# Hybrid encoder step: input columns in a new order, the convolution norm moved to its projection, a first norm that starts from tokens

## The reference

```
mod = silu(c) @ w_ada + b_ada                 # 6 x 1024, for each of two groups
h = rms_norm(x, g_norm1) * (1 + sc1) + sh1
a_in, b_in, q, k, v, qi, ki, wi, gl = split_cols(h @ w_in)
a = a_in[:, :1024] * sigmoid(a_in[:, 1024:])  # GLU
a = causal_dwconv(concat(hist, a), w_dw, b_dw)          # 31 taps
y_a = silu(layer_norm(a, ln_c_g, ln_c_b)) @ w_pa
z = gelu(b_in);  u = z[:, :1024]
vg = layer_norm(z[:, 1024:], ln_v_g, ln_v_b)
y_b = (u * spatial_gate(vg, w_s, b_s)) @ w_pb           # 128 x 128 masked mixing in 8 groups
q, k = rms_norm(q, g_q), rms_norm(k, g_k)
score = sum_h wi * relu(qi @ ki^T)                      # indexer: picks up to 256 keys a query
o = softmax(q @ k^T - slope * dist, on the picked keys) @ v;  y_c = o @ w_pc
m = sigmoid(gl)[0] * y_a + sigmoid(gl)[1] * y_b + sigmoid(gl)[2] * y_c
x = x + g1 * (m @ w_o)
x = x + g2 * (squared_relu(modulated rms_norm(x) @ w_1 + b_1) @ w_2 + b_2)
```

## Time and profile before

| | us |
|---|---|
| median of 3 runs (2717.16 to 2717.63) | 2717.55 |
| the profiled execution | 2716.72 |
| its span | 2714.9 |
| PE busy | 2508.3 (92%) |
| DVE busy | 1237.8 (46%) |
| POOL busy | 1223.2 (45%) |
| ACT busy | 676.9 (25%) |

### The profile page before, as it was taken

The page is one execution under the profiler, slowest core; times in us unless marked ns, Lnnn a source line. Parts: engine busy times, 40 slices in busy tenths (PEclk is TensorE's granted clock), DMA queues, the critical chain, the costliest instruction groups (busy, mean ns, idle before and its releaser), DMA issues.

```text
span 2714.9 us, 37116 instructions
## 1 busy us (share of the span) xinstructions
PE 2508.3 (92%) x14178; PEld 2345.9 (86%) x14178; DVE 1237.8 (46%) x2190; ACT 676.9 (25%) x824; POOL 1223.2 (45%) x611
## 2 busy tenths in 40 slices
PE   7798979999999997968789999999799999999998
PEld 7698858999999996946344999998699999999998
DVE  1421259999999995154667112211521222222212
ACT  2222463222444234212545100001401100100110
POOL 2532201222988564810222455555644544554552
PEclk7799989999999999965899999999899999999999
DMA  7112202332232232123100457441011111111112
GB/s 273 34 51 61 92 27 70 116 116 86 96 96 85 91 96 93 55 67 100 32 16 5 146 179 244 142 150 39 24 48 36 47 50 38 39 50 43 38 43 86
DMA packets 241682, 217.22 MB, mean 80 GB/s; under 512 B 10529, under 2 KB 220547, under 8 KB 241341
## 3 DMA queue, kind: packets, MB, share of 16 engines
q1 hardware_dynamic: 205780, 127.29, 15.8%
q10 hardware_dynamic: 35817, 88.84, 9.5%
HBM read 163.90 MB, written 52.20 MB: 80 GB/s over the span
## 4 chain that ended last, share of the span: by engine, by line
PE 62%; issue 20%; DVE 7%; POOL 7%; ACT 2%; DMA 1%; SPq 0%; POOLq 0%; DVEq 0%; ACTq 0%
PE acc L1683 52%; PE acc L1977 2%; POOL st L625 1%; POOL wlo L580 1%; PE acc L1651 1%; DVE mx L1535 1%; POOL whi L535 1%; PE acc L1928 1%; PE acc L1695 1%; PE acc L1952 1%; POOL wlo L590 1%; PE acc L1923 1%; DVE st L1531 1%; DVE probs L1531 1%; DMA x1T<-xT_d 0%
## 5 line engine op out<-in xcount | busy, mean ns | idle before, releaser
L1683 PE MATMUL acc<-xa,whi 128*128 128x364 f32 x4176 | 1045.4, 332 | 11.6 <-ACT zT L915 5.4
L1683 PEld LDWEIGHTS acc<-xa,whi 128*128 128x128 f32 x4176 | 747.4, 190 | 20.1 <-issue 17.7
L1683 PE MATMUL acc<-xa,wlo 128*128 128x364 f32 x2088 | 690.4, 331 | 0.0
L1683 PE MATMUL acc<-xb,whi 128*128 128x364 f32 x2160 | 534.9, 329 | 2.7 <-POOL wlo L538 2.7
L535 POOL TENSOR_TENSOR whi<-raw,one 128x1024 fp32r<-128x1024 f32 (+2 forms) x153 | 241.4, 1577 | 514.2 <-PE acc L1683 510.2
L1683 PEld LDWEIGHTS acc<-xa,wlo 128*128 128x128 f32 x2088 | 396.8, 190 | 0.0
L1683 PE MATMUL acc<-xf,whi 128*128 128x364 f32 x1536 | 382.1, 330 | 6.3 <-issue 6.3
L1683 PEld LDWEIGHTS acc<-xb,whi 128*128 128x128 f32 x2160 | 383.1, 188 | 3.0 <-POOL wlo L538 3.0
L1683 PE MATMUL acc<-xb,wlo 128*128 128x364 f32 x1080 | 354.8, 328 | 0.0
L538 POOL TENSOR_TENSOR wlo<-raw,whi 128x1024 fp32r<-128x1024 f32 (+2 forms) x153 | 313.6, 2050 | 12.0
L1683 PEld LDWEIGHTS acc<-xf,whi 128*128 128x128 f32 x1536 | 273.0, 189 | 6.6 <-issue 6.6
(11 more groups left out here) (273 smaller groups left out, 2809.7 us busy)
## 6 DMA issues: line engine op xcount, KB each, us to landing
raw<-in_w_in_dram SPq DMA_DIRECT2D x72, 512.0 KB, 4.1
wmod<-in_w_ada_dram SPq DMA_DIRECT2D x32, 512.0 KB, 4.4
...
gate_d<-st ACTq DMA_DIRECT2D x24, 546.0 KB, 2.8
st<-gate_d ACTq DMA_DIRECT2D x24, 546.0 KB, 4.9
m_d<-st ACTq DMA_DIRECT2D x16, 546.0 KB, 3.6
st<-m_d ACTq DMA_DIRECT2D x16, 546.0 KB, 5.9
```

What stands on the lines that cost most here:

```text
L1683: last = nc.tensor.matmul(acc[0:m, s, c, 0:CW], w[:, s, k, 0:m], x[:, half, k, CW * c:CW * (c + 1)], start=(k == 0 and p == 0), stop=(k == ...
```

## The change

- The columns of the input projection are taken in another order: indexer, scores, GLU, gates, the first four u tiles (`UA`), then k, v, q, then VG, then the other four u tiles (`UB`). The convolution's sums are made beside the first u tiles; the means of the convolution stand ahead of VG, those of v between the second and the third tile of UB.
- The convolution's rows go to `ya_d` raw. Mean and root go to `ml_d` and are loaded again before PC; in PB, DVE subtracts and multiplies each row, and ACT does Swish and the rounding.
- The weight tiles of u, k, v, q and VG are rounded by ACT (`round_next`); POOL makes the remainder.
- The first head means of k wait for the convolution (`conv_ok`), because the buffers are shared.
- In the mix DVE multiplies from PSUM, and the copy on ACT is gone. The bias comes by a matmul over eight partitions. The six additions of the distance to the masks (L1444) go into the mask's last step.
- At the start SP loads x first, then the first weights and `w_ada`; the 15 parameter loads are ACT's. ACT squares x by tokens with a sum in the same instruction, DVE evicts all transposes. Conditioning is made in four groups of 16 matmuls of 256 columns, two groups ahead of the first projection and one each behind its rows 1 and 3; ACT scales and shifts the rows.

```diff
-N_GLU = N_Q + H
-N_GATE = N_GLU + 2 * KT
-N_U = N_GATE + 3 * KT
-N_VG = N_U + KT
-N_PC = N_VG + KT
+N_VG = N_Q + H
+N_UB = N_VG + KT
...
+            sp.dma_start(x_tile(0), x_rows[0]).then_inc(x_ld[0], 16)
+            for i, to in enumerate((st[:, 1:3, 0:D], x_mid[:, 0:2, :], x_mid[:, 2:4, :])):
+                rows_of = x_prompt[0, P * (2 * i + 1):P * (2 * i + 3), :]
+                sp.dma_start(to, rows_of.rearrange("(t p) d -> p t d", p=P)).then_inc(x_ld[i + 1], 16)
+            for t in (7, 8):
+                sp.dma_start(x_tile(t), x_rows[t]).then_inc(x_ld[4], 16)
...
+            for q in range(ADA1 // 2):
+                for s in (q, ADA1 // 2 + q):
+                    sp.dma_start(wada[:, s], v_ada[:, :, 2 * P * s:2 * P * (s + 1)]).then_inc(ada_ld[s], 16)
...
-            load_run(N_KV, win, 2 * NKV, C_K)
-            load_run(N_Q, win, H, C_Q)
...
-            load_run(N_U, win, KT, C_U)
+            load_run(N_U, win, UA, C_U)
+            load_run(N_KV, win, 2 * NKV, C_K)
+            load_run(N_Q, win, H, C_Q)
             load_run(N_VG, win, KT, C_V)
+            load_run(N_UB, win, KT - UA, C_U + UA * P)
...
+            def c_sums(n):
+                for m, part in enumerate((apad[:, SUM_ROWS[n], 0:NT], stage(3 + n % 2))):
+                    pool.wait_ge(ln_sq, n + 1)
+                    pool.wait_ge(c_add, 2 * n + m + 1)
+                    total = (sum_a, sum_b)[m][:, :]
+                    nc.gpsimd.tensor_tensor(total, total, part, ALU.add).then_inc(c_add, 1)
...
+            act.dma_start(st[0:CONV_W, 3, 0:D], w_dw[0]).then_inc(par_ld, 16)
...
+                ins = nc.scalar.activation(acc[0:rows(t), 1, 0:2, :].rearrange("p c n -> p (c n)"), x_tile(t), ACT.Square,
+                                           accum_out=ssq[0:rows(t), t:t + 1])
...
+            def partial_sums(q):
+                for s in range(2):
+                    act.wait_ge(ada_mm, 4 * q + s + 1)
+                    nc.scalar.activation(msb1[:, s, :], aux[:, s, 0:2 * P], ACT.Copy).then_inc(mod_cp, 1)
+            def shifted(k):
+                h = 1 + 3 * (k % 2)
+                act.wait_ge(xn_ok, k + 1)
+                act.wait_ge(mod_ok, 2 * (k // 2) + 2)
+                if k > 1:
+                    act.wait_ge(h_lo, k - 1)
+                for g, (a, b) in enumerate(((0, SEQ), (SEQ, NT))):
+                    ins = nc.scalar.activation(st[:, h, a:b], st[:, 2 * (k % 2), a:b], ACT.Identity,
+                                               bias=mod[:, g, M_SH1 + k:M_SH1 + k + 1], scale=gain1[:, g, k:k + 1])
+                ins.then_inc(h_ok, 1)
+                act.wait_ge(h_ok, k + 1)
+                nc.scalar.activation(xa[:, 0, k, :], stage(h), ACT.Copy).then_inc(h_hi, 1)
+            partial_sums(0)
+            partial_sums(1)
+            for q in range(ADA1 // 2):
+                for k in (2 * q, 2 * q + 1):
+                    shifted(k)
+                if q + 2 < ADA1 // 2:
+                    partial_sums(q + 2)
...
+            def round_next(n, s):
+                act.wait_ge(w_load[s], 8 * (n - s) + 32)
+                nc.scalar.activation(whi[:, s], raw[:, s], ACT.Copy).then_inc(w_hi, 1)
...
+                    row = apad[:, SUM_ROWS[n], 0:NT]
+                    wait(act, c_add, 2 * n if n > 1 else 0)
+                    nc.scalar.activation(stage(3 + n % 2), row, ACT.Square).then_inc(ln_sq, 1)
+                    act.dma_start(ya_d[SUM_ROWS[n]], row).then_inc(ya_st, 16)
...
+            def qk_tile(n, s, idx):
+                act.wait_ge(prod, n + 1)
+                round_next(n, s)
...
+                if k == 1:
+                    act.wait_ge(ln_ok, 1)
+                    for m in range(2):
+                        act.dma_start(ml_d[m], stage(2 + m)).then_inc(ml_st, 16)
...
-                        nc.scalar.activation(mixed[:, j, a:b], acc[:, j, m, 0:b - a], ACT.Copy).then_inc(mix_ev, 1)
...
-                        act.wait_ge(br_ld[j], 16 * (i + (KT // 2 * b + 1)))
+                        if b == 0:
+                            act.wait_ge(br_ld[j], 16 * (i + 1))
+                        else:
+                            act.wait_ge(lnc_n, 2 * i + (j + 1))
+                            row = st[:, 2 + j:3 + j, 0:NT]
+                            nc.scalar.activation(row, row, ACT.Silu, bias=par[:, bass.ds(2 * i + (R_LCB + j), 1)],
+                                                 scale=par[:, bass.ds(2 * i + (R_LCG + j), 1)]).then_inc(lnc_s, 1)
+                            act.wait_ge(lnc_s, 2 * i + (j + 1))
...
+            for m, to in enumerate((mean_c, rstd_c)):
+                act.dma_start(to[:, :], ml_d[m]).then_inc(ml_ld, 16)
...
+            def scaled(k):
+                if k > 1:
+                    dve.wait_ge(h_ok, k - 1)
+                nc.vector.tensor_tensor(stage(2 * (k % 2)), xT[:, k, :], acc[:, 1, :, :].rearrange("p c n -> p (c n)")[:, 0:NT],
+                                        ALU.mult).then_inc(xn_ok, 1)
+            dve.wait_ge(x_evd, TT + 1)
+            dve.wait_ge(sq_mm, 1)
+            scaled(0)
+            scaled(1)
+            for q in range(ADA1 // 2):
+                conditioning(q)
+                if q:
+                    scaled(2 * q)
+                    scaled(2 * q + 1)
...
-            with dve.Fori(0, KT // 2) as i:
-                for j in range(2):
-                    row = apad[:, bass.ds(2 * i + j, 1), 0:NT]
-                    nc.vector.tensor_tensor(row, row, st[:, 2:3, 0:NT], ALU.subtract).then_inc(lnc_c, 1)
-                    dve.wait_ge(lnc_c, 2 * i + (j + 1))
-                    nc.vector.tensor_tensor(row, row, st[:, 3:4, 0:NT], ALU.mult).then_inc(lnc_n, 1)
...
-                    nc.vector.tensor_tensor(row, row, mixed[:, j, 0:NT], ALU.mult).then_inc(yb_ok, 1)
+                    nc.vector.tensor_tensor(row[:, 0:TOK], row[:, 0:TOK], acc[:, j, :, :].rearrange("p c n -> p (c n)")[:, 0:TOK],
+                                            ALU.mult).then_inc(yb_ok, 1)
...
+                        if b == 1:
+                            row = st[:, 2 + j:3 + j, 0:NT]
+                            dve.wait_ge(br_ld[j], 16 * (i + (KT // 2 + 1)))
+                            nc.vector.tensor_tensor(row, row, mean_c[:, :].unsqueeze(1), ALU.subtract).then_inc(lnc_c, 1)
+                            dve.wait_ge(lnc_c, 2 * i + (j + 1))
+                            nc.vector.tensor_tensor(row, row, rstd_c[:, :].unsqueeze(1), ALU.mult).then_inc(lnc_n, 1)
...
-            def first_modulation(m):
-                pe.wait_ge(ada_ld[m // 2], 16)
-                for k in range(KT):
-                    last = nc.tensor.matmul(acc[:, 0, 0, 2 * m:2 * m + 2], wada[:, m // 2, k, P * (m % 2):P * (m % 2 + 1)],
-                                            cT[:, :, k], start=(k == 0), stop=(k == KT - 1))
-                if m % 2:
-                    last.then_inc(ada_mm, 1)
...
+            def conditioning(q):
...
+                for s, chunk in ((0, q), (1, ADA1 // 2 + q)):
+                    pe.wait_ge(ada_ld[chunk], 16)
+                    for k in range(KT):
+                        c = k % 4
+                        last = nc.tensor.matmul(aux[32 * c:32 * (c + 1), s, 0:2 * P], cpad[:, k, :], wada[:, chunk, k, :],
+                                                start=(k < 4), stop=(k >= 4))
+                    last.then_inc(ada_mm, 1)
+                for s in range(2):
+                    pe.wait_ge(mod_cp, 2 * q + s + 1)
+                    for h in range(2):
+                        last = nc.tensor.matmul(aux[:, s, 2 * P + 2 * h:2 * P + 2 * h + 2], msb1[:, s, P * h:P * (h + 1)],
+                                                sel[:, :], start=True, stop=True)
...
-            gemm_as_ready(N_KI, 0, xa, h_lo, 0, KIW)
+            conditioning(0)
+            conditioning(1)
+            for k in range(KT):
+                if k == 0:
+                    pe.wait_ge(w_split, N_KI + 1)
+                pe.wait_ge(h_lo, k + 1)
+                for c in range(CH):
+                    for p, (w, half) in enumerate(((whi, 0), (whi, 1), (wlo, 0))):
+                        last = nc.tensor.matmul(acc[0:KIW, 0, c, 0:CW], w[:, 0, k, 0:KIW], xa[:, half, k, CW * c:CW * (c + 1)],
+                                                start=(k == 0 and p == 0), stop=(k == KT - 1 and p == 2))
+                if k in (1, 3):
+                    conditioning(k // 2 + 2)
...
             plain(N_KV + 1)
+            pe.wait_ge(conv_ok, POOL_ROWS[0])
             key_means(0)
...
+            for k in range(KT - UA):
+                if k < 2:
+                    pe.wait_ge(ev_act, N_UB + k - 1)
+                elif k == 2:
+                    pe.wait_ge(ev_act, N_UB + 2)
+                    pe.wait_ge(v_add, 2 * KT + 2)
+                    layer_norm_means()
+                    pe.wait_ge(ln_mean, 2)
+                else:
+                    pe.wait_ge(ln_var, 2)
...
```

(47 more changed lines are left out.)

647 lines of the change are left out of this document (294 added, 353 removed).

## The result

The changed kernel takes 2683.64 us (median of four runs, 2681.62 to 2690.5) against 2717.59 of the kernel before beside it: a ratio of 0.9871, with 0.9859 to 0.9883 as its 95% interval, or 34 us less. The forecast was 2698, 20 less. The profiled execution took 2681.62, its span 2679.7; PE's last matmul ends at 2676.24, and at 2711.41 before: 35.2 to account for.

The account below looks back on a forecast made before the run. PE was taken to set the end, by its matmuls where full and its waits elsewhere. From 2716.72, -26 (start) -7 (order) -2 (mix) +15 (PB) = -20 gave 2696.7, with 0.83 to the median 2697.5, forecast 2698; own range 2682 to 2713.

Parts of the forecast that it names:

- PB: Second branch projection: convolution-norm subtract and multiply on DVE close a loop, turn 14.4 over PE's 12.0; +15 us.
- Start: Before the first index-query tile: x loaded first, squares on ACT, conditioning in groups; 94 us against 119.7, -26.
- the break: In the start, ACT's row loop waits for partial sums of conditioning groups 2 and 3; 8.5 us each, 17 together.
- The rival of a start that gives little: Start: parameters late beside x, breaks of 15; first index-query tile at 112 in place of 94, total 2716; chance 0.12.
- Order: New column order, from the end of the index-query tiles to the mix: 1007.8 us against 1015.3, -7.
- The 8 added for twelve more tiles to round: First head means to last q tile: 8 us added for ACT rounding twelve more weight tiles and a 0.94 clock.
- the stall: After the two k tiles, PE waits 17.5 us for the convolution and the sums whose buffers the k norm uses.
- nothing makes the convolution end sooner against the scores: New order: DVE's convolution keeps its distance from the scores while PE arrives earlier, eating most of the norms' gain; total -7.
- Mix: Spatial mix: PSUM copy goes, DVE multiplies from PSUM, evictions stay; half clock, gain between 0 and 7.7, -2 us.
- the rival of a full clock: Spatial mix holds full clock behind twelve full gemms: about 60 us for 84.9, total 2675; chance 0.17.
- The rival of 19: Second branch projection: DVE's new instructions meet POOL every turn, turn 19, cost +45 to +49, total 2729; chance 0.15.
- Taken at nothing: Attention, output projection and MLP keep their instructions, and the reload of the two statistics lies beside other work: 0 us.

## Why the prediction was right

The sign, the mechanisms of the start, the mix and PB, and the order of the terms held; the sum was 15 short, from terms that were sized too dear and from a search that ran shorter by chance.

- **Start**, -26 forecast, -29.0. The parameters came at 21.37 for 18, the first row at ACT at 50.48 for 50, so what lies between took 29.1 for 32. From there to the first index-query tile it took 40.2 for 43.4: the mis-sized term is the break, about 7.2 where 8.5 was taken, twice. The rival of a start that gives little (112) is out.
- **Order**, -7 forecast, -14.6. The scores took 63.6 for 55.9, since POOL's work on the GLU weights now comes in among them, behind SP's wait for the outputs; the forecast named no such move. The 8 added for twelve more tiles to round was not needed: v to the last q tile took 179.3 for 186.7. That these two cancel is luck. Most of what is left lies between GLU's start and the head means, 595.1 for 601.4: GLU (220.2 for 221.8), the gate, u and k tiles (360.8 for 362.1) and the stall (14.1 for 17.5). VG with its rest took 157.1 for 158. Here "nothing makes the convolution end sooner against the scores" did not hold in the profiled execution: the convolution ends 583.3 after GLU's start, and ended 589.6 after it before. The search's tiny instructions took 31.7 for 39.1, and the forecast had no term for that. Where they took 38.3, in the run without the norm in PB, the whole stretch was 1005.9: -9.4, near the forecast. So some 5 of the 14.6 hang on how the search and POOL happened to meet. The rest of the step holds: a gain of PE between the scores and the k tiles is eaten (PE stood idle for 33.7 in the two LayerNorm stretches, and 14.1 came back at the k tiles).
- **Mix**, -2 forecast, -3.3. Its clock is 0.51, the lower level of 1.2 GHz, also behind full gemms at 0.98, so the rival of a full clock is out; the waits for evictions in it fell from 7.7 to 5.2, and the start alone left it at 85.0.
- **PB**, +15 forecast, +11.6. The turn was forecast at 14.4 with 1.30 an instruction, and measured 14.04: eight subtractions from 1559.52 to 1657.77, over seven. The closed loop is shown by the row loaded ahead, which gives 11.1 of it back. A wait of 1.5 for POOL's remainder ahead of the next branch's second tile, which that run doesn't have either, belongs to it too: 13.1 in all. The rival of 19 is out: POOL is done before each row lands.
- **Taken at nothing**: attention and its projection gave 3.5, and what follows PB took 3.5 more, 1.5 of it the wait just named. For attention it is PE's busy time that fell, 188.1 to 185.6 for the same 665 matmuls, with a granted clock of 0.91 for 0.90, and in its projection from 98.3 to 97.1, with 0.98 for 0.97. Why the clock was granted so, and the other 2.0 behind PB, stays open.

The forecast's own range, 2682 to 2713, holds the time near its low end.
